# Expert stage with 64-slot units: where the outputs' scaling and the next rows' halves stand between the weight pieces

## What is computed

```
def run_block(args):
    xblk, e = args
    h = jax.nn.silu(xblk @ w1[e]) * (xblk @ w3[e])
    return h @ w2[e]
...
y_assign = yb[dest] * gate.reshape(-1)[order][:, None]
return jax.ops.segment_sum(y_assign, tok_sorted, num_segments=T)
```

## Time and profile before

| what | us |
|---|---|
| median of 3 runs | 2112.51 |
| lowest and highest of them | 2105.33, 2122.25 |
| the profiled execution's own time | 2105.5 |
| its span, first to last instruction | 2103.7 |

### The profile page before, as it was taken

The page is one execution under the profiler, slowest core; times in us unless marked ns, Lnnn a source line. Parts: engine busy times, 40 slices in busy tenths (PEclk is TensorE's granted clock), DMA queues, the critical chain, the costliest instruction groups (busy, mean ns, idle before and its releaser), DMA issues. The chain is left out here.

```text
span 2103.7 us, 76229 instructions
## 1 busy us (share of the span) xinstructions
PE 1710.5 (81%) x31174; PEld 1373.8 (65%) x31176; DVE 1465.6 (70%) x1828; ACT 1066.9 (51%) x1378; POOL 527.3 (25%) x413
## 2 busy tenths in 40 slices
PE   3488889888579996999941789985898799999947
PEld 0366666434267775455531689985898799999942
DVE  2576766488869997788878546776886636577737
ACT  2234343677468886433302445565666435466516
POOL 0000000000047776433312013321322212223213
PEclk7699999999889999999965899997999899999979
DMA  9321211476363332344415767898998858789737
GB/s 375 98 91 60 90 60 51 157 236 217 130 251 110 119 119 67 121 142 147 147 67 204 261 208 248 277 311 309 351 373 285 273 148 265 245 283 353 248 72 278
DMA packets 167293, 412.59 MB, mean 196 GB/s; under 512 B 15977, under 2 KB 24625, under 8 KB 165553
## 3 DMA queue, kind: packets, MB, share of 16 engines
q1 hardware_dynamic: 155554, 369.14, 49.1%
q0 software_dynamic: 11664, 42.47, 8.3%
HBM read 343.38 MB, written 68.19 MB: 196 GB/s over the span
## 5 line engine op out<-in xcount | busy, mean ns | idle before, releaser
L2198 PE MATMUL ps<-arena 128*128 128x64 f16 x7680 | 708.4, 196 | 84.9 <-DVE arena L2150 41.4
L2198 PEld LDWEIGHTS ps<-arena 128*128 128x128 f16 x7680 | 688.3, 100 | 87.6 <-issue 70.7
L2199 PE MATMUL ps<-arena 128*128 128x64 f16 x7680 | 708.2, 196 | 1.8 <-issue 1.8
L2200 PE MATMUL ps<-arena 128*128 128x64 f16 x7680 | 708.0, 196 | 0.3 <-issue 0.2
L2199 PEld LDWEIGHTS ps<-arena 128*128 128x128 f16 x7680 | 688.1, 100 | 3.4 <-issue 2.6
L2200 PEld LDWEIGHTS ps<-arena 128*128 128x128 f16 x7680 | 688.1, 100 | 2.2 <-issue 2.2
L2117 DVE SCALAR_TENSOR_TENSOR arena<-arena 128x2048 f16<-128x2048 f32 (+1 forms) x232 | 458.7, 2013 | 214.8 <-ACT arena L2041 138.7
L2041 ACT ACTIVATE arena<-arena 128x2048 f16<-128x2048 f32 x192 | 359.5, 1904 | 168.6 <-DMA arena<-w 111.7
L643 PE MATMUL ps<-arena 128*128 128x256 f16 (+1 forms) x1680 | 238.1, 303 | 21.0 <-DVE arena L528 21.0
L643 PEld LDWEIGHTS ps<-arena 128*128 128x128 f16 x1680 | 165.4, 99 | 87.9 <-DVE arena L528 15.2
L2008 POOL COPY ix<-gidx 128x1 int32 (+1 forms) x40 | 55.7, 1392 | 546.9 <-DVE arena L2150 546.9
(11 more groups left out here) (308 smaller groups left out, 3101.4 us busy)
## 6 DMA issues: line engine op xcount, KB each, us to landing
arena<-w SPq DMA_DIRECT2D x192, 1024.0 KB, 8.4
arena<-hT_d SPq DMA_DIRECT2D x64, 512.0 KB, 6.0
arena<-w_mod SPq DMA_DIRECT2D x16, 1536.0 KB, 8.4
h_d<-arena SPq DMA_DIRECT2D x17, 512.0 KB, 3.0
x_d<-arena SPq DMA_DIRECT2D x17, 512.0 KB, 2.6
arena<-x SPq DMA_DIRECT2D x8, 1024.0 KB, 6.8
hT_d<-arena SPq DMA_DIRECT2D x16, 512.0 KB, 3.1
arena<-x SPq DMA_DIRECT2D x16, 512.0 KB, 4.7
```

The costliest lines, as they stand in the source:

```text
L2198: pe.matmul(out, whi[lane][:, at:at + P], high, start=first, stop=False)
L2199: pe.matmul(out, whi[lane][:, at:at + P], low, start=False, stop=False)
L2200: return pe.matmul(out, wlo[lane][:, at:at + P], high, start=False, stop=last)
```

## The change

On ScalarE, w3's pieces of both lanes follow `x_high(n+1)`, and the wait for lane 0's half of `up3(n)` is gone. On DVE, `scale_y(n-2)` stands ahead of w1's pieces of lane 0 (behind w2's), and w3's pieces of both lanes follow `x_low(n+1)`. In the prologue `x_high(0)` and `x_low(0)` stand ahead of w3's pieces of lane 0. SyncE, GpSimd and TensorE are as they were.

```
@@ ScalarE's step @@
                 silu(n)
                 with act.If(fresh[1] == 1):
                     split(0, 1, own[1])
-                with act.If(fresh[0] == 1):
-
-                    act.wait_ge(up3_mm, START + 2 * n + 1)
-                    split(1, 0, both[0])
                 x_high(n + 1)
-                with act.If(fresh[1] == 1):
-                    split(1, 1, both[1])
+                for lane in range(2):
+                    with act.If(fresh[lane] == 1):
+                        split(1, lane, both[lane])
                 h_high(n)
             for lane in range(2):
                 split(0, lane, 0)
+            x_high(0)
             split(1, 0, 0)
-            x_high(0)
             split(1, 1, 1)
@@ DVE's step @@
-                fresh, own, both = starts(dve, n + 1)
-                with dve.If(fresh[0] == 1):
-                    split(0, 0, own[0])
                 if at_least(n, 2):
                     scale_y(n - 2)
-                with dve.If(fresh[1] == 1):
-                    split(0, 1, own[1])
-                with dve.If(fresh[0] == 1):
-                    split(1, 0, both[0])
+                fresh, own, both = starts(dve, n + 1)
+                for lane in range(2):
+                    with dve.If(fresh[lane] == 1):
+                        split(0, lane, own[lane])
                 hidden(n)
                 x_low(n + 1)
-                with dve.If(fresh[1] == 1):
-                    split(1, 1, both[1])
+                for lane in range(2):
+                    with dve.If(fresh[lane] == 1):
+                        split(1, lane, both[lane])
                 h_low(n)
             dve.wait_ge(g2_ld, START + 16)
             for lane in range(2):
                 split(0, lane, 0)
+            x_low(0)
             split(1, 0, 0)
-            x_low(0)
             split(1, 1, 1)
```

## The result

The changed kernel took 2098.13 us in the median (2096.75 to 2101.49, 8 runs) against 2113.46 (2105.33 to 2122.25, 8 runs): a ratio of 0.9927, 95% interval 0.9909 to 0.9946. Its profiled execution took 2099.6 us, span 2097.8.

What follows compares the result with a forecast made beforehand. TensorE was taken to set the pace where no weights are late, with late weights behind its other waits. Losses of 10.5 us less gains of 10.4 gave +0.1 us on the median 2112.5: 2112.6 us, range 2102 to 2126.

Steps and rivals of the forecast that it cites:

- Step 18: `down(17)` starts 5.4 us earlier and at full clock, `up1(19)` some 0.3 us late: gain 7.1 us.
- Steps 33 to 35: Earlier scaling and low halves of x gain 2.7 us, earlier gathered rows in step 34 0.6 us.
- the four waits of the earlier trace: `down` for the scaling, 1.16 and 0.84 us, `up1(34)` and `up1(36)` for `x_low`, 0.36 each: all go, 2.7 us.
- The clock: Matmuls slow after long idle time: `up3(11)` 0.4, `up3(13)` 0.3, `up3(21)` 1.9, `up3(0)` some 1.5, together 4.1 us lost.
- The prologue: Lane 0's w3 low halves end 2.0 us later, delaying `up3(0)`, which also runs some 1.5 us slower.
- the shift: Lane 0's w3 frees the stage later, delaying lane 1's w3: 1.7, 1.0, 1.7 us in steps 10, 12, 20, prologue 2.0.
- +7.0 us in steps 10, 12 and 20: Losses where both lanes are fresh next: 1.7 + 1.0 + 1.7 us of hand-over and 2.6 us of clock.
- a rival in which GpSimd is late: Low halves right behind the scaling delay scatter and gather; steps 18, 33, 35 lose 6 us: 2118 us, chance 0.10.
- the hand-over: Lane 0's w3 low half frees the shared stage, then lane 1's w3 load is issued and lands, followed by its cast.
- all of its 6.4 us: Bound on the hand-over's loss, 1.7 + 1.0 + 1.7 + 2.0 us, which the time from low half to landing could absorb.
- the rival of 2102: W3 loads wait for the DMA queue, not their issue; losses vanish, 10.4 us stay: 2102.1 us, chance 0.14.

Runs made afterwards that it cites:

- ctl_before: The kernel before, unchanged, timed again against itself with a second profile: ratio 1.0012.
- same_before: The kernel before, unchanged, run again beside the whole change and its two halves on another chip: ratio 0.9989.
- only_w3: The kernel before with only w3's pieces of both lanes moved behind `x_high` and `x_low`; scaling and prologue stay: ratio 0.9996 to the kernel before.
- after_late: The changed kernel with GpSimd's scatter held back until `hidden` of its step: ratio 1.0000 to the kernel before.
- before_late: The kernel before with GpSimd's scatter held back until `x_low` of that step: ratio 1.0128 to the kernel before.

## Why the prediction was wrong

- **Step 18, 7.1 us: held.** Measured 7.4. `down(17)` started 0.45 us behind its predecessor (forecast about 0.5), at full clock.
- **Steps 33 to 35, 3.3 us: held.** Measured 3.4, the four waits of the earlier trace rows and the one for gathered rows gone.
- **The clock: held.** `up3(21)` paid 1.3 us, `up3(11)` took 6.7 us instead of 7.3, and both pay 0.9 us in the transposes ahead of them, where the slow stretch now begins (1.97 us instead of 1.09). That makes 2.2 and 0.3 us, forecast 1.9 and 0.4.
- **The prologue, 2.0 us and 1.5 of clock: held in the profiles** (2.3 us with the scatter, 3.2 without); in the medians its sign is open.
- **Wrong: "I take the shift one to one, since rows 7 show both casts waiting for these loads."** The shift of the issue is right (1.7 us measured), and it counts one to one if nothing else changes: the pair without the scatter shows that, where the landing stays and the three places lose 8.6 us. But I moved the scaling two pieces ahead in these very steps and asked only what DVE and TensorE have from it. It also releases GpSimd's scatter and, behind it, the gather. These went 6 us further ahead of the loads, their packets were over (within 0.5 us) when the loads were issued, and the loads landed 2.5 and 2.7 us sooner on average. In place of +7.0 us in steps 10, 12 and 20 came -1.5. The text had both pieces (the copy in the earlier trace rows, the scatter behind the scaling), and used them only for a rival in which GpSimd is late.
- **Wrong beneath it: the hand-over was read from one execution that was untypical.** In steps 10 and 20 of the first profile of before the slow copy had put the scatter behind the loads, and they landed at +5.1 and +9.2. In two more profiles it was +7.5 to +8.0 and +11.4 to +12.1. Steps 10, 11 and 20, 21 were 2 to 4 us shorter in it than in the other two, so even this reading hid what could be gained.
- **What the trace "agreed" with.** The rival of the late GpSimd says that the copy ends in the first gap between low halves. The low halves follow each other without a gap, and in other profiles the copy ends with the first of them, not with the fourth (last section).
- **The bound was too narrow.** "The hand-over could absorb all of its 6.4 us" was the best case of my range; that the landing could improve stood nowhere. 10.4 us of gain and nothing lost was the rival of 2102; the measured time lay 4 us under it. That it came so near is partly luck, since the prologue's loss is real and some 5 us are unexplained.
- **Missed, with little cost here:** the long wait comes before `transposes_y`, on `keep_y`, not before `up3`.

Shown: the change's balance hangs on the scatter (12 to 15 us faster with it, 9.4 slower without), and lane 1's w3 lands later the more of the scatter's and the gather's packets run beside its loads. Not shown: why 1 us of such packets can already cost the first piece 2 us. Not tested alone: the gather, since it moved with the scatter in every kernel; the packet times put the scatter beside the first piece and the gather beside the second. Also open: what the whole change is worth in the group where the pair without the scatter was timed, in which it did not run; and some 5 us of the medians that no stretch of the stage holds.

## What to carry to other kernels

When an instruction moves, list what it releases on every engine, above all the DMAs that start behind it, and ask which loads they will then run beside; here a scatter of 0.5 MB that takes 2.8 us of all DMA engines counted for more than the 1.3 us instruction in front of it. Read a term on which the sum rests from a second place or execution: one step in which a helper engine was starved gave a landing 2.5 us off. And leaving the suspected traffic out of both versions told cause from company, where delaying it also delayed a gather that TensorE needed.

## What the runs showed of the hardware

- **A GpSimd copy of 128 numbers took 1.8 us or 8.4 us in the same step of the same kernel,** with DVE's low halves running beside it in both. The Trainium skill, "GPSIMD Engine Reference" (Key points), has the port that GpSimd shares with VectorE. In each of these cases the copy ended within 0.06 us of the end of a low half: the first in ctl_before, same_before and after, the second in only_w3 (4.04 us), the fourth in the first profile of before. Why it is now the first and now the fourth, in steps 10 and 20 alike, is open. In the first profile the copies sum to 55.7 us before and 45.5 after.
- **The scatter's DMA instruction on GpSimd took from 1.6 to 6.0 us.** It was 1.6 or 2.8 us in most places and 5.43 us in step 10 of after_late (above). The weight loads issued meanwhile don't explain it: some of 1.6 us had two beside them, and that of 6.0 us, in after_late too, had none. Those of 3 us and more had DVE busy for at least 2.6 us beside them; whether that is the cause was not tested.
- **A gap in TensorE's steps, in some executions.** Two matmuls that else follow each other within 0.15 us then lie 0.24 to 0.35 us apart, once or twice a step. Steps 23 to 32 took 190.3 us in after and 186.7 in the first profile of before. It is no matter of the order of work. All profiles of the two groups in which the kernel before had medians of 2101.5 and 2098.4 us lack it (186.7 to 187.6 us, the pair without the scatter among them). Those of the four groups with medians from 2110.3 to 2112.1 have it (189.7 to 191.2, and 199.4 in before_late, which also waits for gathered rows). The first profile of before lacks it too, though that kernel's median was 2113.5 us there. What makes it is open.
- **The level of one and the same kernel differs between groups of runs:** the kernel before had medians from 2098.4 to 2113.5 us, as much as the whole change.
